# Dealing projections beside the sample rows of a hybrid decoder step by explicit counts, with one gate chunk more there and one fewer in the scan

## The reference

```python
h = rmsnorm(x); u = h @ w_in            # one projection, columns split into the parts below
# A: Mamba-2 SSD (z gate, x/B/C with a causal conv of 4, dt; 16 heads x 64, 4 groups, state 128,
#    chunks of 128 tokens, state carried from chunk to chunk), D skip, gated RMSNorm
# B: dilated sliding-window attention, 3 groups (window, dilation) x 8 heads x 64;
#    groups merged per head by their softmax denominators; times silu(z)
# C: cross-attention, 4 heads x 128, into 256 memory tokens; times silu(z)
merged = sum(sigmoid(gate_i) * (y_i @ w_branch_i) for i in A, B, C)
y = rmsnorm(x + merged @ w_out)
```

## Time and profile before

| | |
|---|---|
| median of three runs | 2274.84 us (2265.24, 2274.94, 2274.84) |
| the profiled execution | 2267.2 us |
| its span, first to last instruction | 2265.3 us |
| TensorE busy (matmul) | 2071.6 us, 91% |
| VectorE busy | 1059.1 us, 47% |
| ScalarE busy | 808.6 us, 36% |
| mean granted TensorE clock | 0.946 of full |

### The profile page before, as it was taken

The page is one execution under the profiler, slowest core; times in us unless marked ns, Lnnn a source line. Parts: engine busy times, 40 slices in busy tenths (PEclk is TensorE's granted clock), DMA queues, the critical chain, the costliest instruction groups (busy, mean ns, idle before and its releaser), DMA issues.

```text
span 2265.3 us, 35670 instructions
## 1 busy us (share of the span) xinstructions
PE 2071.6 (91%) x14602; PEld 1967.1 (87%) x14602; DVE 1059.1 (47%) x2065; ACT 808.6 (36%) x1733; POOL 238.7 (11%) x358
## 2 busy tenths in 40 slices
PE   4899998999979999999998789999999978979997
PEld 4799998998869999999998669857999978979997
DVE  5204676425445344443346682464444465445423
ACT  5223353213343233223634112454555463123202
POOL 1000121100001010112122000000211111100000
PEclk9899999999989999999999887999999989999998
DMA  6211232211101121212255575376233355554422
GB/s 209 78 39 58 77 94 69 88 45 47 38 26 63 36 65 37 82 62 67 83 168 172 170 219 165 115 257 195 80 112 114 101 183 152 179 170 161 133 81 102
DMA packets 166994, 248.76 MB, mean 110 GB/s; under 512 B 19701, under 2 KB 114613, under 8 KB 166805
## 3 DMA queue, kind: packets, MB, share of 16 engines
q1 hardware_dynamic: 144576, 179.50, 25.5%
q0 software_dynamic: 22256, 66.98, 9.0%
HBM read 179.73 MB, written 66.70 MB: 109 GB/s over the span
## 4 chain that ended last, share of the span: by engine, by line
PE 77%; DVE 9%; ACT 6%; issue 4%; DMA 3%; SPq 0%; DVEq 0%; POOL 0%; ACTq 0%; POOLq 0%
PE bank L2244 19%; PE bank L2245 19%; PE bank L2246 19%; PE bank L2414 2%; DVE w_lo L1686 2%; PE bank L2389 2%; PE bank L2372 2%; PE bank L2640 1%; ACT soft L1490 1%; ACT w_hi L1355 1%; PE bank L2350 1%; DVE softT L1936 1%; PE bank L2456 1%; PE bank L2482 1%; ACT Lm L1613 1%
## 5 line engine op out<-in xcount | busy, mean ns | idle before, releaser
L2244 PE MATMUL bank<-w_hi,hT_hi 128*128 128x256 f32 (+1 forms) x1872 | 546.6, 292 | 26.7 <-ACT hT_hi L1473 18.8
L2245 PE MATMUL bank<-w_lo,hT_hi 128*128 128x256 f32 (+1 forms) x1872 | 534.0, 285 | 0.0
L2246 PE MATMUL bank<-w_hi,hT_lo 128*128 128x256 f32 (+1 forms) x1872 | 532.8, 285 | 0.0
L2244 PE MATMUL bank<-hT_hi,w_hi 128*128 128x352 f32 x1344 | 459.0, 341 | 16.0 <-DVE w_lo L1686 9.9
L2246 PE MATMUL bank<-hT_hi,w_lo 128*128 128x352 f32 x1344 | 444.9, 331 | 0.0
L2245 PE MATMUL bank<-hT_lo,w_hi 128*128 128x352 f32 x1344 | 444.7, 331 | 0.0
L2244 PEld LDWEIGHTS bank<-w_hi,hT_hi 128*128 128x128 f32 (+1 forms) x1872 | 356.9, 191 | 29.5 <-issue 24.4
L2246 PEld LDWEIGHTS bank<-w_hi,hT_lo 128*128 128x128 f32 (+1 forms) x1872 | 357.5, 191 | 0.9
L2245 PEld LDWEIGHTS bank<-w_lo,hT_hi 128*128 128x128 f32 (+1 forms) x1872 | 356.6, 190 | 0.8
L2244 PEld LDWEIGHTS bank<-hT_hi,w_hi 128*128 128x128 f32 x1344 | 263.7, 196 | 23.5 <-DVE w_lo L1686 10.3
L2245 PEld LDWEIGHTS bank<-hT_lo,w_hi 128*128 128x128 f32 x1344 | 264.2, 197 | 0.8
(11 more groups left out here) (427 smaller groups left out, 3159.1 us busy)
## 6 DMA issues: line engine op xcount, KB each, us to landing
w_raw<-in_w_in SPq DMA_DIRECT2D x96, 512.0 KB, 5.0
kvring<-in_cache_win_kv SPq DMA_DIRECT2D x144, 256.0 KB, 3.4
feat_T<-fstage POOLq DMA_DIRECT2D x40, 528.0 KB, 4.3
fstage<-feat_T SPq DMA_DIRECT2D x16, 528.0 KB, 4.3
kvring<-in_cache_mem_kv SPq DMA_DIRECT2D x32, 256.0 KB, 3.6
xc<-feat_T SPq DMA_DIRECT2D x8, 1024.0 KB, 6.4
o_rows<-obuf POOLq DMA_DIRECT2D x48, 132.0 KB, 2.0
mo<-o_rows SPq DMA_DIRECT2D x24, 264.0 KB, 3.6
```

Of the source, the lines that this page charges most:

```text
L2244: pe.matmul(out, xh(k), wh(k), start=(k == 0), stop=False)
L2245: pe.matmul(out, xh(k), wl(k), start=False, stop=False)
L2246: ins = pe.matmul(out, xl(k), wh(k), start=False, stop=(k == nk - 1))
```

## The change

`spread` no longer deals the fillers of items 1 to 4 above; counts written out do. A new helper `fill(k)` gives the next k projections, and any split that comes ahead of or right behind them, uncounted. There are 4 projections ahead of the first merge; one behind each merge and one behind each transposition; 2 behind the last of these; 2 behind each sprep and each ssoft; one behind every four of the 64 products and one behind every three of the 24 turned sets. What is left is spread over the values, now in groups of four instead of eight. `N_SAMPLE_FILL` is 10 instead of 9, so the scan gets five chunks instead of six. No instruction of any step is altered; only the list's order is.

```diff
--- before.py
+++ after.py
@@ -109,7 +109,7 @@
          'd_skip', 'ssd_norm_w', 'mem_norm_w', 'w_mem_kv', 'w_br_ssd', 'w_br_att', 'w_br_mem', 'w_out', 'norm_f_w']
 
 
-N_MEM_FILL, N_TAIL_FILL, N_SAMPLE_FILL = 8, 2, 9
+N_MEM_FILL, N_TAIL_FILL, N_SAMPLE_FILL = 8, 2, 10
 PASSES = ((1, 4),)
 PASS_AT = {1: 0}
 
@@ -255,27 +255,35 @@
         return steps
 
     steps = gate_steps(N_SAMPLE_FILL)
-    side = [[]] * 7
+
+    def fill(k):
+
+        out = []
+        while steps and (k or steps[0][0][0] == "split"):
+            k -= steps[0][0][0] != "split"
+            out += steps.pop(0)
+        return out
+
+    sched += fill(4)
     for b in range(NB):
-        side += [[("merge", b)], [], [("mturn", b - 1)] if b else [], []]
-    side += [[("mturn", NB - 1)]]
+        sched += [("merge", b)] + fill(1) + ([("mturn", b - 1)] if b else []) + fill(1)
+    sched += [("mturn", NB - 1)] + fill(2)
     for g in range(NG):
-        side += [[("sprep", g)], []]
-    group, weight = [], 0
-    for n, x in enumerate(sets):
-        group.append(("skey", n))
-        weight += 1
-        if weight >= 4:
-            side.append(group)
-            group, weight = [], 0
-    side += [group + [("skey", len(sets))], [("ssoft", 0)], [], [], [("ssoft", 1)], [], [], [("ssoft", 2)], [], []]
+        sched += [("sprep", g)] + fill(2)
+    n_products = sum(x[3] is not None for x in sets)
+    for n in range(len(sets)):
+        sched.append(("skey", n))
+        if n < n_products and n % 4 == 3 or n >= n_products and (n - n_products) % 3 == 2 and n + 1 < len(sets):
+            sched += fill(1)
+    sched += [("skey", len(sets))] + fill(1)
+    for i in range(3):
+        sched += [("ssoft", i)] + fill(2)
     sval = []
     for n in range(len(values)):
         sval.append([("sval", n)])
         sval[-1] += [("sod", x) for x in range(2 * BS) if part_end[x] + 2 == n]
         sval[-1] += [("soT", y) for y in range(5) if part_end[last_part(y)] + 5 == n]
-    side += [sum(sval[i:i + 8], []) for i in range(0, len(sval), 8)]
-    sched += spread(side, steps)
+    sched += spread([sum(sval[i:i + 4], []) for i in range(0, len(sval), 4)], steps)
     steps = gate_steps(1)
     for i, x in enumerate([[("sod", 15)], [("soT", 5)], [("sout", 2)], [], [("ssd_setup",)], [("tail",)], [("ssd_dA",)]]):
         sched += x + steps[i]
```

## The result

Median of 20 runs 2273.09 us (2266.50 to 2281.89), beside 20 runs of the kernel before at 2267.57: a ratio of 1.0031, 95% interval 1.0020 to 1.0042. The change costs 0.3%. The forecast was 2250, with a gain of 19.7 us (0.9%) by its sum; the measured median lies 3 us above the upper end of its range. The profiled execution has a span of 2270.5 us against 2265.3, and that difference of 5.2 is what has to be explained. (The median of three shown before, 2274.84, was high: over 20 runs the kernel before is at 2267.6, the level of its profiled execution.)

The account below looks back on a forecast made before the run. TensorE, holding 77% of the chain that ended last, was taken to bound the kernel. Terms -14 + 2.9 + 0 + 1.6 + 8.5 - 18.7 = -19.7 took 2267.2 to 2247.5 us, forecast as 2250; range 2228 to 2270.

Parts of the forecast that it names:

- Merge: from 101 to about 87: Merge: with eight fewer projections it turns from bound by TensorE to bound by VectorE, -14 us.
- Rivals 1 and 2: Merge: held by its loads and ScalarE, total +2 us (chance 0.09); half clock between merges, total +18 us (0.08).
- Values: +8.5: Value rows: six more projections, +23.2 us of TensorE work, partly fill holes; 100.5 us becomes 109.
- TensorE's work becomes 99: Value rows: TensorE's own work, 76 us before, rises to 99 us with fourteen projections instead of eight.
- with four values to a projection ... both are ready in time: Value rows: VectorE needs only 2.8 us during a 5.7 us group, so ScalarE and VectorE keep up with TensorE.
- the 10 us left for splits and holes: Value rows: 10 us of TensorE holes allowed for three weight splits, eight pairs of value groups without a projection between, and loads.
- Turned keys: +1.6: Turned key sets: three more projections cost +11.9 us, against 10.3 us of half clock won back.
- I take the half clock as gone: Turned key sets: alternating three sets and a projection removes the half clock, which lost 10.3 us before.
- Products: 0: Per-head key products: four more projections fit in TensorE's idle time, so 0 us; bounds -4 and +4.
- Scan: -18.7: Scan chunks 0 to 5: six fewer projections save 23.7 us, less added waits where splits leave no cover; -18.7 us.
- The four places dealt by hand: Scan chunks 1 to 3: places where a split replaces a projection; waits of 2.4, 3, 3.6 and 1, 10 us in all.
- The 33.2 us a chunk: Scan: TensorE's part per chunk with five projections, 13.4 of its own work plus 5 x 3.95, above the chain's 29.7 us.

Follow-up runs that it names:

- early_high: Changed kernel with ScalarE making the high part of the fourth value ahead before it waits to evict a projection among the values; 2268.48 us, 1.0018.
- small_splits: Changed kernel with weight splits among the values handling an eighth of their weights, the rest left unsplit; 2268.32 us, 1.0012.
- lead_values: Changed kernel with each weight split among the values put directly ahead of the next projection, not in a place of its own; 2268.84 us, 1.0023.
- half_value_loads: Changed kernel with each value row's load bringing 64 of its 128 partitions; 2270.94 us, 1.0011.
- counts_only: Changed kernel with nine chunks beside the sample rows and six for the scan: written-out counts, chunk not moved; 2264.14 us, 0.9989.
- split_free_scan: Changed kernel with each weight split tied to the projection before it when the scan's steps are dealt; 2256.26 us, 0.9951.
- lead_join_early: Changed kernel with splits ahead of the next projection in the sample rows, tied behind one in the scan, and the edit of early_high; 2248.78 us, 0.9923.
- keys_pairs: lead_join_early with two projections after every sixth turned key set instead of one after every third; 2253.35 us, 0.9939.

## Why the prediction was wrong

**Right.** *Merge: from 101 to about 87*: 87.5, by the mechanism named. TensorE's first wait was 7.9 us (7.3 forecast) and all its waits for `macc` 14.5 in four. Counts and sprep (+2.5 for +2.9) too. Rivals 1 and 2 didn't come. One bound was wrong by its own timeline: without the 3 us for late loads merge is 84, which is 6 lost, not 4.

**Values: +8.5, was +20.3.** This is the largest miss, and three steps of it failed. First, "TensorE's work becomes 99" left out 16 matmuls that add the new values' part (3.7 us); it is 14 x 3.86 + 88 x 0.47 + 3.7 + some 5 of small steps = 104. The same were left out of the kernel before, so its holes were some 19 us, not 24.5: less could be won. Second, "with four values to a projection ... both are ready in time": ScalarE goes through the list in order and makes the high part three values ahead, so the fourth stands behind the projection's eviction. Only three values are ready when a projection ends, and the rest comes at the pace of ScalarE and VectorE (0.62 and 0.69 us). early_high showed it: 2.48 to 1.85 us for four. Third, the 10 us left for splits and holes are 17: the two runs of twelve blocks, which are dealt where a split takes a place, took 21.1 us to their eleventh, where 22 x 0.47 and four matmuls of the new values are 11.3, and half clock behind the first another 2.6. small_splits and lead_values show that neither the splits' work nor their place alone is the cause; the loads aren't either (half_value_loads), which leaves the depth of three and ScalarE's order, and that was shown only in part: all remedies together took 4 of the 17 us with 14 projections. With 17 and 20 of them no half clock is left. Six projections, 23.2 us of work, added 20.3, so that the dealing in fours saved only some 3.

**Turned keys: +1.6, was +8.1.** The step that failed is "I take the half clock as gone". It was read from one stretch at 1.00 with four sets to a projection; a like alternation, with three sets, fell to half clock in the changed kernel. Of the eight projections there in the changed kernel's timeline four took 5.5 to 6.0 us instead of 3.95. By the mean clocks of the stretch, 0.79 and 0.91, half clock cost an estimated 13.7 us before (0.21 x 65.4) and 6.6 after (0.09 x 73.4): half of it went, where the forecast took back 10.3. TensorE stood idle for 4.1 us instead of 1.7, of which 2.8 are waits for `softT` beside a split. Some 1 us is unexplained, and the same code took 70.3 to 76.3 us in other runs.

**Products: 0, was +3.6.** Within its bounds. VectorE has three splits there instead of two and waits for ScalarE's half before each (10.0 us in three in sprep and products, the longest 7.4). That isn't the cause, though: counts_only has the same sixteen projections, three splits and 8.4 us of such waits, and took 96.3. The clock differs, 0.93 there and 0.88 here, an estimated 5 us of half clock; why is open. With the splits led the stretch is 95.2 with the same sixteen projections: four more projections did fit for nothing, as counted.

**Scan: -18.7, was -10.6.** The mechanism was the one named; the term that was mis-sized is the waits, 15.0 us instead of 10 (against 6.4 before, not 5). The four places dealt by hand came at 2.4, 2.1, 3.3 and 0.9 us (2.4, 3, 3.6 and 1 forecast); a fifth, 4.2 us behind a split in chunk 5, was missed (ScalarE had waited 8.5 us for that chunk's weights to land). Half clock was given no price: at 0.96 instead of 0.98 it is an estimated 8.6 us instead of 4.5. Without these places the same six projections were worth 25.1. The 33.2 us a chunk that the prediction had for TensorE came out once every step was covered: 33.0 to 33.1 in split_free_scan's chunks 1 to 3. So the chain, put at 29.7, didn't bind with five chunks; with four no run decides it.

**Up to the scan: 0, was -5.3.** Not looked at: before, the clock was 0.87 there, and ScalarE waited 3.4 us for a weight load; after, it was 0.98, and ScalarE waited for none.

**The sum.** Values +11.8, scan +8.1, turned keys +6.5, products +3.6, and -5.3 up to the scan: 24.7 of the 25 us between forecast and result. Each of the three large terms was set nearer to its good bound. Values and scan together (19.9) are as large as the whole gain in the sum. What the experiments show is that the moved chunk, as dealt, is the loss, and that with the scan's splits tied the move costs nothing. Half clock was priced only once, in the turned keys, and taken as gone there.

**What stays open.** Why the clock falls behind one stall of 1.5 to 2 us and not behind another, and in one run of key sets and not in a longer one; and what the rest of the 12 us above TensorE's 104 is in the values of lead_join_early, beyond some 7 beside the splits. Loads are not ruled out there: ScalarE waits 16.1 us for them (6.1 in the changed kernel), and half_value_loads was tried on the changed kernel alone.

## What to carry to other kernels

When fillers are dealt over steps, deal only those that cover: a step that itself takes time on the engines being waited for should ride with a filler, not take one's place. In the scan that was worth 14.5 us (216.0 to 201.5); in the values, by itself, nothing. When one engine's order holds both an eviction and the producer of the next work, what is ready after a long filler is what was issued ahead of that eviction; count that depth before pricing a hole. And price half clock as a term of its own, from a stretch's length and mean clock, before and after.

## What the runs showed of the hardware

TensorE's clock fell to its lower level with TensorE never idle. Windows of keys_pairs in the turned keys, columns as in the earlier trace rows: six sets behind one pair of projections, then the first three and the last three sets behind the next pair.

```profile
1373.40:1381.00 7.60, 7.60 (x73) 7.60 (x71) 1.25 (x2) 3.01 (x6) 0.00 (x0) 1.00 0.60 152
1388.90:1392.70 3.80, 3.80 (x37) 3.80 (x36) 0.69 (x1) 1.79 (x5) 0.53 (x1) 1.00 0.55 180
1392.70:1400.10 7.40, 7.40 (x39) 7.40 (x38) 2.04 (x3) 2.40 (x2) 0.00 (x0) 0.50 0.52 169
```

All three are back-to-back small matmuls; in the last the granted clock is 0.50, 1.2 GHz, and a set takes 2.46 us instead of 1.28, while the six sets of the first row all ran at 2.4 GHz. The next projection took 5.2 us and the one after it 3.9. The Trainium skill (TensorE: Matmul & The Clock Gate, "What's actually happening") gives idleness as what brings the lower clock back, and says that the clock goes by how busy the engine has recently been. If idle means a pause between instructions, this trace doesn't agree: TensorE was busy for 7.40 of 7.40 us, and the row decides. What the chip itself counts as busy these rows can't tell.
